# Expert choice by comparing all pairs of logits, half of a tile turned before the router, index work in three pieces inside the first item

## The reference

```python
logits = (xt @ router_w).astype(jnp.float32)
top_vals, top_idx = lax.top_k(logits, TOP_K)
top_p = jax.nn.softmax(top_vals, axis=-1)
gates = jnp.sum(jax.nn.one_hot(top_idx, N_EXPERTS) * top_p[..., None], axis=1)
for e in range(N_EXPERTS):
    out = out + gates[:, e:e + 1] * swiglu(xt, w13[e], w2[e])
```

## Time and profile before

| | |
|---|---|
| median of 3 runs | 1541.32 us (1540.59 to 1542.39) |
| the profiled execution | 1545.48 us, span 1543.6 us |
| PE busy | 1482.8 us, 96% of the span |
| DVE, ACT busy | 1187.6 us (77%), 976.2 us (63%) |
| POOL busy | 35.2 us (2%) |
| mean granted clock of PE | 0.982 of 2.4 GHz |
| chain of waits that ended last | PE 91%, DVE 5%, ACT 1%, DMA 1% |

### The profile page before, as it was taken

How to read it: one execution, slowest core, us unless ns; L and a number is a source line. 1 busy time by engine, 2 the same in 40 slices (tenths; PEclk the granted TensorE clock), 3 DMA queues, 4 the chain that set the end, 5 groups by cost and what they waited for, 6 DMA issues and landing times.

```text
span 1543.6 us, 21457 instructions
## 1 busy us (share of the span) xinstructions
PE 1482.8 (96%) x7403; PEld 1245.6 (81%) x7403; DVE 1187.6 (77%) x1053; ACT 976.2 (63%) x932; POOL 35.2 (2%) x53
## 2 busy tenths in 40 slices
PE   7999899999999979999999999999999999999992
PEld 6989778887989768888888888888888888888882
DVE  6676644536477478889889889888888888888884
ACT  6445534435445457777777777777777777777772
POOL 1000000000000001000000000000000000000001
PEclk9999999999999989999999999999999999999996
DMA  8738545444535339999999999999999999999983
GB/s 296 291 137 315 186 177 196 178 177 149 194 110 204 110 118 415 389 378 384 375 373 402 366 375 388 370 380 390 371 378 394 369 377 401 372 367 388 378 317 111
DMA packets 69179, 464.80 MB, mean 301 GB/s; under 512 B 7629, under 2 KB 9053, under 8 KB 16264
## 3 DMA queue, kind: packets, MB, share of 16 engines
q1 hardware_dynamic: 61688, 437.22, 73.7%
q0 software_dynamic: 7440, 26.91, 4.7%
HBM read 456.36 MB, written 16.12 MB: 306 GB/s over the span
## 4 chain that ended last, share of the span: by engine, by line
PE 91%; DVE 5%; issue 1%; ACT 1%; DMA 1%; POOLq 0%; ACTq 0%; POOL 0%; DVEq 0%; SPq 0%
PE bank L1210 29%; PE bank L1212 28%; PE bank L1211 28%; PE bank L1544 2%; DVE w_lo L764 1%; PE bank L1253 1%; DVE xn L804 1%; PE bank L1327 0%; PE bank L1394 0%; PE bank L1337 0%; PE bank L1325 0%; PE bank L1533 0%; DMA g_row<-in_mix_norm_g 0%; DMA bias<-done,row_i 0%; PE bank L1414 0%
## 5 line engine op out<-in xcount | busy, mean ns | idle before, releaser
L770 DVE TENSOR_TENSOR w_lo<-raw,w_hi 128x2048 fp32r<-128x2048 f32 x333 | 762.1, 2292 | 103.2 <-ACT w_hi L478 99.9
L478 ACT ACTIVATE w_hi<-raw 128x2048 fp32r<-128x2048 f32 x333 | 637.5, 1917 | 124.4 <-PE bank L1212 124.4
L1210 PE MATMUL bank<-w_hi,yT_hi 128*128 128x512 f32 x1528 | 606.0, 397 | 6.5 <-DVE yT_lo L776 3.6
L1212 PE MATMUL bank<-w_hi,yT_lo 128*128 128x512 f32 x1528 | 598.1, 391 | 0.0
L1211 PE MATMUL bank<-w_lo,yT_hi 128*128 128x512 f32 x1528 | 597.1, 391 | 0.0
L1210 PEld LDWEIGHTS bank<-w_hi,yT_hi 128*128 128x128 f32 x1528 | 288.5, 189 | 68.5 <-DVE w_lo L770 5.4
L1212 PEld LDWEIGHTS bank<-w_hi,yT_lo 128*128 128x128 f32 x1528 | 288.2, 189 | 61.5
L1211 PEld LDWEIGHTS bank<-w_lo,yT_hi 128*128 128x128 f32 x1528 | 288.7, 189 | 57.7
L764 DVE TENSOR_TENSOR w_lo<-raw,w_hi 128x1024 fp32r<-128x1024 f32 x160 | 188.5, 1220 | 57.2 <-ACT w_hi L472 55.5
L472 ACT ACTIVATE w_hi<-raw 128x1024 fp32r<-128x1024 f32 x160 | 160.5, 1054 | 40.3 <-PE bank L1212 38.0
L776 DVE TENSOR_TENSOR yT_lo<-bank,yT_hi 128x512 fp32r<-128x512 f32 (+1 forms) x94 | 62.3, 679 | 54.0 <-ACT yT_hi L529 48.8
(11 more groups left out here) (214 smaller groups left out, 917.5 us busy)
## 6 DMA issues: line engine op xcount, KB each, us to landing
raw<-in_moe_units SPq DMA_DIRECT2D x336, 1024.0 KB, 7.1
raw<-in_layer_units SPq DMA_DIRECT2D x44, 1024.0 KB, 4.9
raw<-in_dense_units SPq DMA_DIRECT2D x33, 1024.0 KB, 4.9
sent<-in_x POOLq DMA_DIRECT2D x1, 6144.0 KB, 35.1
xn<-sent POOLq DMA_DIRECT2D x9, 512.0 KB, 8.0
done<-qk POOLq DMA_DIRECT2D x8, 512.0 KB, 8.9
done<-in_x POOLq DMA_DIRECT2D x1, 2048.0 KB, 41.8
x<-in_x SPq DMA_DIRECT2D x2, 512.0 KB, 3.7
```

What stands on the lines that cost most here:

```text
L478: act.activation(w_hi[:, st.split(u), :, :].rearrange("p a n -> p (a n)"), raw[:, st.slot(u), :], ACT.Copy)\
L770: dve.tensor_tensor(w_lo[:, st.split(u), :, :].rearrange("p a n -> p (a n)"), raw[:, st.slot(u), :], w_hi[:, st.split(u), :, :].rearrange( ...
L1210: pe.matmul(out, hi_l, hi_r, start=start, stop=False, skip_group_check=True)
L1212: return pe.matmul(out, lo_l, hi_r, start=False, stop=stop, skip_group_check=True)
```

## The change

PE turns the first half of tile 1 before the router's products of tile 0, into bank 6; the second half stays between the tiles. On DVE the root of tile 0 moves behind the last gain multiply, and the first half of unit 23 is split after the root of tile 1. The choice compares every pair of logits of a token: `above` and `level` are 2 x 8 x 8 numbers in each row, `earlier` (made in the cross-attention stage) lets an equal logit with a lower index count as above, and the number of logits above gives each expert's place. Masks are places 0 and 1. The selection matrix comes before the gates. The index work keeps only `over` in its old place; its other parts are functions that DVE runs inside item 0 at the ends of steps 1, 2 and 3. The core of the diff:

```diff
@@ -989,6 +994,8 @@
                 dve.wait_ge(sem("router_in"), 32)
+                c.step(dve.tensor_tensor(earlier[:, :, :], less8[:, 0, :].unsqueeze(1).broadcast_to([P, NE, NE]),
+                                         less8[:, 0, :].unsqueeze(2).broadcast_to([P, NE, NE]), ALU.is_lt))
@@ -1041,16 +1048,16 @@
                 times_gain(1, 0)
-                root(m, 0, told=True)
                 turned_lo(m, 0, (4, 5), xT_hi, xT_lo)
...
                 half_means(m, 1)
-                lo(st, 23, which=(0,))
+                root(m, 0, told=True)
                 turned_lo(m, 1, (6, 7), xT_hi, xT_lo)
                 root(m, 1, told=True)
+                lo(st, 23, which=(0,))
@@ -1086,34 +1093,37 @@
-        pick_first(top[:, 0, :], top[:, 3, :], sel1[:, :, :])
-        c.link(dve.scalar_tensor_tensor(lg[:, :, :], sel1[:, :, :], -3e38, lg[:, :, :], ALU.mult, ALU.add))
-        pick_first(top[:, 4, :], top[:, 5, :], sel2[:, :, :])
-
-        dve.tensor_tensor(top[:, 1, :], top[:, 4, :], top[:, 0, :], ALU.subtract).then_inc(sem("top_diff"), 1)
-        dve.tensor_tensor(mask_h[:, :, :], sel1[:, :, :], sel2[:, :, :], ALU.add).then_inc(sem("mask"), 1)
-        c.link(dve.tensor_tensor(mask[:, :, :], sel1[:, :, :], sel2[:, :, :], ALU.add))
+        shape = [P, NT, NE, NE]
+        other, own = lg[:, :, :].unsqueeze(2).broadcast_to(shape), lg[:, :, :].unsqueeze(3).broadcast_to(shape)
+        c.step(dve.tensor_tensor(level[:, :, :, :], other, own, ALU.is_ge))
+        c.step(dve.tensor_tensor(above[:, :, :, :], other, own, ALU.is_gt))
+        c.wait()
+        c.link(dve.tensor_tensor(level[:, :, :, :], level[:, :, :, :], earlier[:, :, :].unsqueeze(1).broadcast_to(shape),
+                                 ALU.mult))
+        c.link(dve.tensor_tensor(above[:, :, :, :], above[:, :, :, :], level[:, :, :, :], ALU.max))
+        c.link(dve.tensor_reduce(place8[:, :, :], above[:, :, :, :], AX.X, ALU.add))
+        dve.tensor_scalar(mask_h[:, :, :], place8[:, :, :], 1.0, None, ALU.is_le).then_inc(sem("mask"), 1)
+        c.step(dve.tensor_scalar(mask[:, :, :], place8[:, :, :], 1.0, None, ALU.is_le))
+        c.step(dve.tensor_scalar(sel1[:, :, :], place8[:, :, :], 0.0, None, ALU.is_equal))
+        c.step(dve.tensor_scalar(sel2[:, :, :], place8[:, :, :], 1.0, None, ALU.is_equal))
+        c.wait()
+        c.link(dve.tensor_tensor(place8[:, :, :], sel2[:, :, :], sel1[:, :, :], ALU.subtract))
+        c.link(dve.tensor_tensor(place8[:, :, :], place8[:, :, :], lg[:, :, :], ALU.mult))
+        dve.tensor_reduce(top[:, 1, :], place8[:, :, :], AX.X, ALU.add).then_inc(sem("top_diff"), 1)
+        dve.wait_ge(sem("rank_mm"), 1)
+        c.link(dve.scalar_tensor_tensor(tmp8[:, :, :], rank, 1.0, mask[:, :, :], ALU.add, ALU.mult))
+        for t in range(NT):
+            last = dve.tensor_scalar(S[:, t, :], iota, 1.0, tmp8[:, t, 0:1], ALU.add, ALU.is_equal)
+        last.then_inc(sem("select"), 1)
+        dve.wait_ge(sem("select"), 1)
+        c.step(dve.tensor_scalar(tmp8[:, :, :], tmp8[:, :, :], -1.0, None, ALU.add))
         dve.wait_ge(sem("top_exp"), NT)
...
@@ -1126,30 +1136,38 @@
-        c.link(dve.tensor_scalar(over[:, :], bank[3][:, 0:NE], float(P), None, ALU.is_gt))
...
+        c.step(dve.tensor_scalar(over[:, :], bank[3][:, 0:NE], float(P), None, ALU.is_gt))
+        def own_blocks():
+            c.step(dve.tensor_scalar(base[:, :], less8[:, 0, :], float(P), float(NE * P), ALU.mult, ALU.add))
+            c.step(dve.tensor_scalar(lg[:, :, :], tmp8[:, :, :], float(P), None, ALU.is_ge))
+            c.link(dve.tensor_reduce(first[:, 0:1], over[:, :], AX.X, ALU.add))
...
+        def second_blocks():
+            for k in range(OVER):
+                c.link(dve.tensor_tensor(pick[:, k, :], over[:, :], less8[:, 0, :], ALU.mult))
...
+        def rows_of_tokens():
+            c.link(dve.tensor_tensor(lg[:, :, :], lg[:, :, :], base[:, :].unsqueeze(1).broadcast_to([P, NT, NE]), ALU.mult))
...
+            dve.tensor_copy(row_i[:, :, :], row[:, :, :]).then_inc(sem("rows_known"), 1)
...
@@ -1176,6 +1194,12 @@
+                if first and j == 1:
+                    own_blocks()
+                if first and j == 2:
+                    second_blocks()
+                if first and j == 3:
+                    rows_of_tokens()
@@ -1496,6 +1523,7 @@
+        turn_half(m, 1, 0, 6)
         for t in range(NT):
...
             if t == 0:
-                turn_tile(m, 1, (6, 7))
+                turn_half(m, 1, 1, 7)
```

More of the change, by code:

```diff
@@ L275, in _build @@
     done = nc.dram_tensor("done", [(ITEMS + 1) * P, D], F32, kind="Internal").ap()
+    above = pool_a[:, 0, 0:NT * NE * NE].rearrange("p (t a b) -> p t a b", t=NT, a=NE)
+    level = pool_a[:, 1, 0:NT * NE * NE].rearrange("p (t a b) -> p t a b", t=NT, a=NE)
+    earlier = pool_b[:, 0, 0:NE * NE].rearrange("p (a b) -> p a b", a=NE)
+    place8 = pool_b[:, 1, 0:NT * NE].rearrange("p (t e) -> p t e", t=NT)
     mean, half_mean, lnv, r0, newton, rstd = (norm_s[:, i, :] for i in range(6))
@@ L1087, in _ @@
         c.link(dve.tensor_reduce(lg[:, :, :], parts, AX.X, ALU.add))
[L1089 to L1095, removed]
@@ new lines, in _ @@
+        c.link(dve.tensor_tensor(place8[:, :, :], place8[:, :, :], lg[:, :, :], ALU.mult))
+        dve.tensor_reduce(top[:, 1, :], place8[:, :, :], AX.X, ALU.add).then_inc(sem("top_diff"), 1)
+        dve.wait_ge(sem("rank_mm"), 1)
+        rank = bank[1][:, 0:NT * NE].rearrange("p (t e) -> p t e", t=NT)
+        c.link(dve.scalar_tensor_tensor(tmp8[:, :, :], rank, 1.0, mask[:, :, :], ALU.add, ALU.mult))
+        dve.wait_ge(sem("mats_in"), 16)
+        for t in range(NT):
+            last = dve.tensor_scalar(S[:, t, :], iota, 1.0, tmp8[:, t, 0:1], ALU.add, ALU.is_equal)
@@ L1107, in _ @@
         c.link(dve.tensor_tensor(top[:, 6, :], top[:, 2, :], top[:, 7, :], ALU.mult))
[L1109 to L1116, removed]
         lo(layer_stream(DEPTH - 1), 23, which=(1,))
@@ L1151, in _ @@
-        c.link(dve.tensor_scalar(first[:, 1:OVER + 1], first[:, 1:OVER + 1], float(NE), float(NE - 1), ALU.add, ALU.min))
-        dve.tensor_copy(info[0:1, :], first[0:1, :]).then_inc(sem("info_ready"), 1)
+        c.step(dve.tensor_scalar(over[:, :], bank[3][:, 0:NE], float(P), None, ALU.is_gt))
[3 more added lines that the diff above has]
+            c.link(dve.tensor_reduce(first[:, 0:1], over[:, :], AX.X, ALU.add))
+            c.link(dve.tensor_scalar(first[:, 0:1], first[:, 0:1], float(NE), None, ALU.add))
+            c.link(dve.tensor_tensor(tmp8[:, :, :], tmp8[:, :, :], base[:, :].unsqueeze(1).broadcast_to([P, NT, NE]),
+                                     ALU.add))
+            c.link(dve.tensor_scalar(base[:, :], base[:, :], -1.0, None, ALU.mult))
@@ new lines, in second_blocks @@
+        def second_blocks():
+            for k in range(OVER):
+                c.link(dve.tensor_tensor(pick[:, k, :], over[:, :], less8[:, 0, :], ALU.mult))
+                c.link(dve.tensor_reduce(first[:, k + 1:k + 2], pick[:, k, :], AX.X, ALU.min))
+                c.link(dve.tensor_scalar(pick[:, k, :], less8[:, 0, :], first[:, k + 1:k + 2], None, ALU.is_equal))
+                c.link(dve.tensor_tensor(over[:, :], over[:, :], pick[:, k, :], ALU.subtract))
+                c.link(dve.scalar_tensor_tensor(base[:, :], pick[:, k, :], float((NE + k - 1) * P), base[:, :],
+                                                ALU.mult, ALU.add))
@@ new lines, in rows_of_tokens @@
+        def rows_of_tokens():
+            c.link(dve.tensor_tensor(lg[:, :, :], lg[:, :, :], base[:, :].unsqueeze(1).broadcast_to([P, NT, NE]), ALU.mult))
+            c.link(dve.tensor_tensor(tmp8[:, :, :], tmp8[:, :, :], lg[:, :, :], ALU.add))
+            for k, chosen in enumerate((sel1, sel2)):
+                c.link(dve.tensor_tensor(lg[:, :, :], chosen[:, :, :], tmp8[:, :, :], ALU.mult))
+                c.link(dve.tensor_reduce(row[:, k, :], lg[:, :, :], AX.X, ALU.add))
+            dve.tensor_copy(row_i[:, :, :], row[:, :, :]).then_inc(sem("rows_known"), 1)
+            c.link(dve.tensor_scalar(first[:, 1:OVER + 1], first[:, 1:OVER + 1], float(NE), float(NE - 1), ALU.add, ALU.min))
+            dve.tensor_copy(info[0:1, :], first[0:1, :]).then_inc(sem("info_ready"), 1)
@@ L1246, in features_out, with turn_half @@
                 mm.then_inc(sem("unit_used"), 1)
+        def turn_half(m, t, half, b):
+            pe.wait_ge(sem("xn_ready"), m * 4 + 2 * t + half + 1)
+            for k in range(4):
+                a = (4 * half + k) * P
+                mm = pe.transpose(bank[b][:, k * P:(k + 1) * P], xn[:, t, a:a + P], ident)
+            mm.then_inc(sem("xT_mm"), 1)
         def turn_tile(m, t, banks):
             for half in range(2):
[L1250 to L1254, removed]
+                turn_half(m, t, half, banks[half])
         def turned(m, t, half):
```

## The result

The changed kernel took 1549.26 us (median of 7 runs, 1546.2 to 1550.87) against 1541.32 (7 runs, 1537.15 to 1542.58): the ratio is 1.0054, with a 95% interval of 1.0042 to 1.0067. That is 7.9 us slower, outside the forecast range. Its profiled execution took 1549.78 us with a span of 1547.9.

The account below looks back on a forecast made before the run. PE bounds the loop at full clock; before it, a chain of small DVE instructions delays PE's gather. Terms -1.2 -4.4 +2.0 +0.4 +2.5 +1.7 give +1.0 us on the median 1541.32: 1542.3, range 1537.5 to 1546.0.

Parts of the forecast that it names:

- the mask: Router's choice on DVE: in the changed profile the mask comes 1.7 us after the logits.
- the selection: Router's choice on DVE: in the changed profile the selection comes 1.2 us after the mask.
- the stalls of about 2.0 and 0.4: Loop: PE idles about 2.0 us before the unit following the second index piece, 0.4 after the third, none after the first.
- the row turn released by a late fetch: Item 1's row turn (L1533): released by the fetch, with a scatter of over 2 us ahead.
- Turning earlier: Router's stage, half of the second tile turned earlier: 0.1 us gained, between nothing and 0.6, as PE finds DVE busy.
- Choosing by pairs: DVE chain from logits to selection: gains of 0.88 us up to the mask and 0.56 from mask to select.
- The gather: PE's gather of rows: starts 1.5 us sooner, partly lost at half clock; 1.2 gained, between 0.7 and 2.4.
- The stall before unit 3: PE's wait while DVE does index work: its removal gains 2.65 us, 4.4 with the low clock after it.
- The three pieces: Index work at the ends of loop steps: first piece costs nothing, second stalls PE 2.0 us, third 0.4.
- What waits for the indices: POOL's four scatters, then item 1's row fetch: late fetch stalls PE 2.5 us at the turned rows, ends 0 and 5.
- The clock: Low clock behind the two long stalls, 0.6 likely for each: one low stretch of the two possible, costing 1.7 us.
- The losing rival: Turned rows: all four scatters held, 4.1 us stall, both long stalls lower the clock; +4.3, 1545.6 us; chance 0.23.

Follow-up runs that it names:

- the last experiment: Changed kernel with index work cut finer into DVE's gaps, plus the first half of unit 23 split behind the selection, not ahead of the logits: 1536.35 us, ratio 0.9969.
- pieces_back: Changed kernel with all index work back in its old place ahead of unit 3; pair choice and earlier turning stay: 1539.36 us, ratio 0.9995.
- rows_behind_turn: Changed kernel with the third piece of index work behind the subtraction of the turned hidden tile instead of ahead of it: 1546.33 us, ratio 1.003.
- two_steps_more: Changed kernel with two more small DVE steps, read by nobody, behind the turned tile's subtraction in step 4: 1538.78 us, ratio 0.9986.
- spread_only: Kernel before the change with only the index work moved, in three pieces, to the ends of steps 1, 2 and 3: 1550.65 us, ratio 1.0074.
- dve_waits: Changed kernel with DVE waiting behind the third piece for POOL's signal from behind the line issuing the first scatter: 1539.47 us, ratio 0.999.
- all_step1: Changed kernel with all three pieces of index work at the end of step 1: 1541.99 us, ratio 1.001.
- cast_last: Changed kernel with the table of items made ahead of the row numbers' cast: one run, 1547.87 us.

## Why the prediction was wrong, by its steps

Every sign that it named came: the mask, the selection, the stalls of about 2.0 and 0.4, and the row turn released by a late fetch. One term of the sum was far too small.

- **Turning earlier (0.1)**: right. From the last sum (L816, 544.15; now L821, 541.24) to the logits it was 6.07 and is 5.95. The reason given, the half unit on DVE, was half of it, as the last experiment shows.
- **Choosing by pairs (0.88 and 0.56)**: right. The mask came 1.73 behind the logits (forecast 1.71), the selection matrix 1.14 behind the mask (1.16), and the comparison of 128 elements took 0.29, near the 0.28 read from L1115. Two details of the reading were off and changed nothing: from L1087 to the mask there were thirteen starts and not twelve (0.20 each), and with twice L1115 for each dependent step the chain comes to 2.67, a loss of 0.1 and not of 0.5.

```profile
547.19 0.19 DVE L1094 TENSOR_REDUCE lg<-bank 128x16 f32<-128x32 f32 x1
547.42 0.29 DVE L1099 TENSOR_TENSOR pool_a<-lg 128x128 f32<-128x128 f32 x1
...
548.92 0.17 DVE L1106 TENSOR_SCALAR mask_h<-pool_b 128x16 bf16<-128x16 f32 x1
...
550.06 0.48 DVE L1119 TENSOR_SCALAR prob<-mats,tmp 128x128 f32<-128x128 f32 x2
```

- **The gather (1.2 net)**: right. It starts 1.56 sooner and takes 5.92 for 5.74, so 1.4 in this execution.
- **The stall before unit 3 (2.65, with the clock 4.4)**: gone, as said; the granted clock is 1.00 from 556.6 to 609.7. The 1.7 of the clock in it depend on the execution: behind 2.52 us of the same stall in `pieces_back` the clock stayed at 1.00.
- **The three pieces (0, 2.0, 0.4)**: right. PE's idle time is none, 1.85 and 0.21, where the same way of counting gave 2.51 for the 2.65, so 2.0 and 0.35.
- **What waits for the indices (2.5, ends 0 and 5)**: the mechanism was the right one and the size was off by 5.4. Here the prediction failed. It let the first scatter in "behind the first unit after the third piece", because the two held ones before had got in at the next boundary between units. The first was held over two more boundaries: 7.42 in place of 3.0, 4.4 us more. A smaller share is the data of the scatters, 7.96 on average between them for the forecast 7.78, and 8.4 for the fetch in place of 8.0. The other three scatters took 4.97 together, no more than I had given them. In `rows_behind_turn`, where the first scatter was held to one boundary only (2.44), the wait is 4.52; in `two_steps_more`, where it was not held, the wait is gone.
- **The clock (one low stretch of two, 1.7)**: both came in the profiled execution, 1.7 and 1.9. The first is a draw, as `spread_only` and `two_steps_more` show (1.00 behind the same stall).

With what was measured put into the sum: -1.6 +0.2 (the gather itself) -4.4 +2.0 +0.4 +7.9 +3.6 = +8.1, against the 7.9 of the medians. So close a match is in part luck, since the clock's terms differ from one execution to the next. The losing rival had the mechanism, the place and the sign, and stopped at +4.3, since it too went by boundaries; it was the right case with the wrong upper end. I gave it 0.23. What I could have seen: two holds in a trace of four scatters are too few for a rule about when a hold ends, and in a chain where each link waits for the one before, an end of 5 us for a run of DVE 6.7 long left out the plain bound, one whole run.

## What to carry to other kernels

When work is moved to where an engine has idle time, follow its result to the last reader, through every queue in between: from the cast to PE's turning there were 108.5 us, of which four scatters in a chain and the fetch took 38.9 + 8. 2.8 of the 38.9 were holds, so that 61.6 us were free with them and 64.4 without; the cast was moved by 63.4 by the prediction's count. That is in time only if nothing at all is held, which `two_steps_more` and `dve_waits` came near enough to, and the changed kernel did not. Lay small work against the idle time and the measured lead of each unit, in pieces no longer than both together. Where POOL issues indirect transfers beside DVE's long subtractions of two SBUF tiles, bound its wait by the whole run of them and not by one.

## What the runs showed of the hardware

An indirect transfer issued by POOL took 0.96 to 1.02 us when it began ahead of one of DVE's unit subtractions or at the very end of one, 1.8 to 3.1 when it was held to the end of one, and 7.15 to 7.42 when it was held through a run of three without a gap; it ended 0.9 to 1.0 after the run in the four kernels in which that happened (the changed one, `spread_only`, `all_step1`, `cast_last`). The plain fetch took 0.57 beside the same subtractions. The Trainium skill, in its GPSIMD Engine Reference, Key points, says that POOL contends with VectorE's instructions that have two SBUF inputs; the traces agree, and here it comes to a factor of seven. The data of the first scatter landed sooner, 4.86 and 5.04 us after POOL's instruction, in the two kernels in which it was not held, against 6.57 or more in all others; No run here shows why. The granted clock of TensorE fell behind an idle time of 1.85 us in four traces (mean 0.80 over the next 8.4 us) and stayed at 1.00 behind the same idle time in two.
